# A streaming encoder step: expert rows are weighted out of PSUM and added onto the residual rows by indirect DMA

## What is computed

```
m = silu(c) @ w_ada + b                        # shift, scale, gate, for each request
h = LN0(x) * (1 + scale_m) + shift_m
x = LN_m(alpha * x + gate_m * mixer(h))        # "x1" below
h = LN0(x) * (1 + scale_f) + shift_f           # "h2" below
# each token: one of 4 groups, 2 of its 4 experts, weights w0 and w1
for e in range(16):
    a = silu(h @ w_gate[e]) * (h @ w_up[e])    # 1024 -> 512
    y = y + combine[:, e:e+1] * (a @ w_down[e])
x = LN_f(alpha * x + gate_f * y)               # gate_f: one row for prompt, one for sample
```

## Time and profile before

| | us |
|---|---|
| median of 3 runs | 1449.58 |
| the three runs | 1443.32, 1449.58, 1452.94 |
| the profiled execution, its own time | 1447.76 |
| its span | 1445.2 |

### The profile page before, as it was taken

The page is one execution under the profiler, slowest core; times in us unless marked ns, Lnnn a source line. Parts: engine busy times, 40 slices in busy tenths (PEclk is TensorE's granted clock), DMA queues, the critical chain, the costliest instruction groups (busy, mean ns, idle before and its releaser), DMA issues.

```text
span 1445.2 us, 19719 instructions
## 1 busy us (share of the span) xinstructions
PE 1286.7 (89%) x7193; PEld 994.2 (69%) x7194; DVE 799.4 (55%) x1042; ACT 589.2 (41%) x780; POOL 335.2 (23%) x449
## 2 busy tenths in 40 slices
PE   2897999999999989999999988999999999999900
PEld 0654678787787756656687876887777888887700
DVE  5624132323422065676689975556888251548678
ACT  0422012322212166676722132555777242447532
POOL 0122230001200065675535631000000000000073
PEclk8899999999999999999999998999999999999955
DMA  9755210102031171121323369666999261649773
GB/s 338 285 175 176 62 67 0 59 1 73 1 95 41 46 207 30 31 59 31 121 99 117 109 237 374 230 225 241 388 389 382 104 232 58 232 149 378 273 253 123
DMA packets 138775, 234.52 MB, mean 162 GB/s; under 512 B 57328, under 2 KB 58936, under 8 KB 138712
## 3 DMA queue, kind: packets, MB, share of 16 engines
q1 hardware_dynamic: 128440, 196.41, 38.6%
q0 software_dynamic: 6496, 23.60, 4.7%
q10 hardware_dynamic: 3776, 13.67, 2.3%
HBM read 197.96 MB, written 35.68 MB: 162 GB/s over the span
## 4 chain that ended last, share of the span: by engine, by line
PE 58%; issue 12%; DVE 8%; ACT 5%; POOL 5%; DMA 1%; ACTq 1%; POOLq 0%; DVEq 0%
PE psum L819 53%; POOL arena L2042 3%; PE psum L1025 2%; ACT high L1464 2%; PE psum L1214 1%; DVE arena L1981 1%; DVE arena L1980 1%; DVE arena L1973 1%; DVE arena L1971 1%; DVE arena L1972 1%; ACT a_high L1496 1%; PE psum L1220 1%; DMA arena<-h_rows,smalls 1%; DVE win_low L1676 0%; PE psum L1119 0%
## 5 line engine op out<-in xcount | busy, mean ns | idle before, releaser
L819 PE MATMUL psum<-win_high,x_high 128*128 128x512 f32 (+1 forms) x432 | 173.8, 402 | 3.5 <-DVE win_low L1676 3.5
L819 PE MATMUL psum<-win_high,x_low 128*128 128x512 f32 (+1 forms) x432 | 170.0, 394 | 0.0
L819 PE MATMUL psum<-win_low,x_high 128*128 128x512 f32 (+1 forms) x432 | 169.9, 393 | 0.0
L819 PE MATMUL psum<-arena 128*64 128x128 f32 (+9 forms) x1324 | 147.0, 379 | 24.6 <-DMA arena<-in_w_ada_mix 20.7
L819 PE MATMUL psum<-high,h_high 128*128 128x512 f32 x416 | 165.1, 397 | 2.5 <-DVE h_low L1927 2.5
L819 PE MATMUL psum<-high,h_low 128*128 128x512 f32 x416 | 163.2, 392 | 0.0
L819 PEld LDWEIGHTS psum<-arena 128*64 128x64 f32 (+6 forms) x1324 | 72.6, 143 | 75.1 <-issue 48.5
L1775 DVE TENSOR_TENSOR_SCAN arena<-arena,psum 128x512 f32<-128x512 f32 (+4 forms) x116 | 109.5, 978 | 19.6 <-ACT arena L1421 19.5
L1922 DVE TENSOR_TENSOR low_odd<-raw_odd,high 128x2048 fp32r<-128x2048 f32 x48 | 107.8, 2288 | 13.7 <-ACT high L1464 13.7
L1922 DVE TENSOR_TENSOR low_even<-raw_even,high 128x2048 fp32r<-128x2048 f32 x48 | 107.7, 2288 | 10.8 <-ACT high L1464 10.8
L2042 POOL TENSOR_TENSOR arena<-arena 128x512 f32<-128x512 f32 (+4 forms) x116 | 108.2, 932 | 9.3
(11 more groups left out here) (257 smaller groups left out, 2437.9 us busy)
## 6 DMA issues: line engine op xcount, KB each, us to landing
raw_even<-in_w_e_gate SPq DMA_DIRECT2D x8, 2048.0 KB, 11.0
raw_even<-in_w_e_up SPq DMA_DIRECT2D x8, 2048.0 KB, 16.5
raw_even<-in_w_e_down SPq DMA_DIRECT2D x8, 2048.0 KB, 14.7
raw_odd<-in_w_e_gate SPq DMA_DIRECT2D x8, 2048.0 KB, 10.5
raw_odd<-in_w_e_up SPq DMA_DIRECT2D x8, 2048.0 KB, 17.0
raw_odd<-in_w_e_down SPq DMA_DIRECT2D x8, 2048.0 KB, 15.1
win<-in_w_in SPq DMA_DIRECT2D x7, 2048.0 KB, 8.0
expert_rows<-arena ACTq DMA_DIRECT2D x26, 512.0 KB, 6.6
```

The source lines that it names most:

```text
L819: pe_last[0] = nc.tensor.matmul(*x, **y)
```

## The change

Parts of the diff, cut to its core. Expert loop, ACT, DVE and POOL:

```diff
@@ ACT, before the loop
+            act.wait_ge(s_ids, 2)
+            act.wait_ge(s_gi, 2)
+            A(slot_w.rearrange("p s b -> p (s b)"), bank(6)[:, 0:2 * MAX_BLOCKS], ACT.Copy).then_inc(s_gi, 1)
+            act.wait_ge(s_gi, 3)
             act.sem_inc(s_ye, 1)
-            act.sem_inc(s_ys, 16)
+            act.wait_ge(s_ys, 16)
+            act.wait_ge(s_router, 128)
@@ ACT, in each block, behind high_parts(nxt, (1, 2, 3))
+                        act.wait_ge(s_ye, b + 1)
+                        A(gate_rows, rows8[:, 1], ACT.Copy, scale=slot_w[:, 1, bass.ds(b, 1)]).then_inc(s_gsA, 1)
                         act.wait_ge(s_yp, b + 1)
-                        act.wait_ge(s_ys, 16 * b + 16)
-                        A(yb.rearrange("p (a c) -> p a c", a=2), psum[2][:], ACT.Copy).then_inc(s_ye, 1)
-                        act.wait_ge(s_ye, b + 2)
-                        act.dma_start(y_dram[bass.ds(b * P, P), :], yb).then_inc(s_ys, 16)
@@ DVE, in each block, behind low_parts(nxt, (1, 2, 3), before) and ahead of low_parts(nxt, (4, 5), before)
+                        dve.wait_ge(s_gsA, b + 1)
+                        STT(gate_rows, rows8[:, 0], slot_w[:, 0, bass.ds(b, 1)], gate_rows, ALU.mult, ALU.add).then_inc(s_gsD, 1)
+                        dve.wait_ge(s_gsD, b + 1)
+                        dve.wait_ge(s_yp, b + 1)
+                        dve.wait_ge(s_ys, 16 * b + 16)
+                        TT(yb, psum[2].rearrange("p a c -> p (a c)"), gate_rows, ALU.mult).then_inc(s_ye, 1)
@@ POOL
+            pool.indirect_dma_start(x1_dram, bass.IndirectOffsetOnAxis(ap=idc[:, 1:2], axis=0), gate_rows, None,
+                                    compute_op=ALU.add).then_inc(s_ys, 16)
             with pool.Fori(1, total + 1) as b:
                 pool.wait_ge(s_htr, b)
                 pool.wait_ge(s_hg, 16 * b)
-                pool.sem_inc(s_fill, 16)
-                G.tensor_copy(idc, gi[:, bass.ds(b, 1)]).then_inc(s_idx, 1)
-                pool.wait_ge(s_idx, b)
+                G.tensor_copy(idc[:, 0:1], gi[:, bass.ds(b, 1)]).then_inc(s_idx, 1)
+                pool.wait_ge(s_idx, 2 * b - 1)
                 pool.sem_inc(s_go, 1)
                 pool.indirect_dma_start(hg, None, h2_dram, bass.IndirectOffsetOnAxis(ap=idc[:, 0:1], axis=0)).then_inc(s_hg, 16)
+                pool.wait_ge(s_ys, 16 * b)
+                G.tensor_copy(idc[:, 1:2], si[:, bass.ds(b - 1, 1)]).then_inc(s_idx, 1)
+                pool.wait_ge(s_idx, 2 * b)
+                pool.wait_ge(s_ye, b + 1)
+                pool.sem_inc(s_go, 1)
+                pool.indirect_dma_start(x1_dram, bass.IndirectOffsetOnAxis(ap=idc[:, 1:2], axis=0), yb, None,
+                                        compute_op=ALU.add).then_inc(s_ys, 16)
```

```diff
@@ DVE, after w0 and w1, ahead of the ranks
+            step(TS(w18, w18, 1.0 / ALPHA, None, ALU.mult))
+            for part in range(3):
+                step(V.tensor_copy(w_part[part], w18 if part == 0 else w_rest))
+                if part < 2:
+                    step(TT(w_rest, w18 if part == 0 else w_rest, w_part[part], ALU.subtract))
@@ POOL, after the gather of block 0
+            for part in range(3):
+                w_of_token = w_part[part].unsqueeze(2).to_broadcast([P, 18, MAX_BLOCKS])
+                G.tensor_tensor(block_w[:, part], block_oh, w_of_token, ALU.mult).then_inc(s_bw, 1)
@@ SP
             sp.wait_ge(s_hg, 16)
+            sp.wait_ge(s_ids, 2)
...
-            with sp.Fori(total, MAX_BLOCKS) as b:
-                sp.dma_start(y_dram[bass.ds(b * P, P), :], zero_rows).then_inc(s_fill, 16)
```

Final stage: the 18 gathers, L1520, L1971, L1972, L1973 and the x1 loads go. SP loads the summed rows in four groups of tiles, (0), (1, 2), (3, 4, 5), (6, 7, 8), once the last add has landed:

```diff
+            sp.wait_ge(s_summed, 1)
+            for i, tiles in enumerate(SUM_GROUPS):
+                for t in tiles:
+                    sp.dma_start(ya[t][0:r], x1_dram[t * P:t * P + r, :]).then_inc(s_sum_in[i], 16)
@@ ACT
-                    A(ya[t][0:r], ya[t][0:r], ACT.Copy, scale=w0[0:r, t:t + 1]).then_inc(s_crs, 1)
+                    A(yc[t][0:r], ya[t][0:r], ACT.Copy, accum_out=fin_nm[0:r, t:t + 1]).then_inc(s_crs, 1)
```

```diff
+                    if j >= 2:
+                        keep_clock((8, 5)[j - 2], 4)
@@ PE, adasum
-                    if i >= 1:
-                        pe.wait_ge(s_rowo, i)
-                    mm(bank(6)[0:2, :], row_of_tile, ada_acc[:, i % 2], start=True, stop=True).then_inc(s_rsum, 1)
+                    if i >= 2:
+                        pe.wait_ge(s_rowo, i - 1)
+                    mm(bank(6 - 2 * (i % 2))[0:2, :], row_of_tile, ada_acc[:, i % 2], start=True, stop=True).then_inc(s_rsum, 1)
```

More of the change, by code:

```diff
@@ L550, in stream_step @@
         an = view(r_b + 17408, 2, 256)
-        zero_rows = view(r_m + EXPERT_W, D)
+        gate_rows = view(r_m + EXPERT_W, D)
+        block_w = view(r_b + 16384, 27 * MAX_BLOCKS).bitcast(BF16).rearrange("p (a n b) -> p a n b", a=3, n=18)
         ya = [view(r_b + D * t, D) for t in range(TILES)]
         yc = [view(r_a + D * t, D) for t in range(TILES)]
-        x1c = [view(r_m + D * t, D) for t in range(TILES)]
         rt = [r_tmp]
@@ L579, in stream_step @@
         dd = rtiny(9)
-        w0 = rtiny(9)
-        w1 = rtiny(9)
+        w01 = rtiny(2, 9)
+        w0, w1 = w01[:, 0], w01[:, 1]
+        w_rest = rtiny(18)
+        w_part = [rtiny(9).bitcast(BF16) for _ in range(3)]
+        slot_w = rtiny(2, MAX_BLOCKS)
         A0 = rtiny(9, 16)
@@ L824, in _, with keep_clock @@
             nc.tensor.transpose(bank(7)[:, 0:72], rows[0:72, :], ident[0:72, 0:72]).then_inc(s_rowT, 1)
+            def keep_clock(n, b=7):
+                for _ in range(n):
+                    mm(bank(b)[:, 0:256], ident, cst[:, 0:256], start=True, stop=True)
             pe.wait_ge(s_silu, 1)
@@ L1151, in _ @@
                     h2_turned(n - 2)
-            def keep_clock(n):
-                for _ in range(n):
-                    mm(bank(7)[:, 0:256], ident, cst[:, 0:256], start=True, stop=True)
             keep_clock(2)
@@ L1197, in _ @@
             pe.wait_ge(s_route, 1)
+            pe.wait_ge(s_gi, 2)
             block_turn(0)
+            for s in range(2):
+                tiles = [n for n in range(18) if (n % 9 == LAST) == bool(s)]
+                for part in range(3):
+                    pe.wait_ge(s_bw, part + 1)
+                    for n in tiles:
+                        r = rows_of(n % 9)
+                        last = mm(bank(6)[:, s * MAX_BLOCKS:(s + 1) * MAX_BLOCKS], place_oh[0:r, n, :], block_w[0:r, part, n, :],
+                                  start=(part == 0 and n == tiles[0]), stop=(part == 2 and n == tiles[-1]))
+            last.then_inc(s_ids, 1)
             with pe.Fori(0, EXPERTS // 2) as ee:
```

199 lines of the change are left out of this document (107 added, 92 removed).

## The result

The changed kernel takes 1554.11 us (median of 4 runs, 1551.86 to 1555.38) against 1447.74 for the kernel before beside it: ratio 1.0748, 95% interval 1.0713 to 1.0783. The forecast was 1487 and 1436 to 1535, so the direction was right and the size far too small. The profiled execution has a span of 1549.7, 104.5 more than before.

What follows compares the result with a forecast made beforehand. PE, busy 89% of the span, was taken to bound the kernel, except in first-projection waits and the 75.3 us after the expert loop. 1447.8 − 30 − 11 + 0 + 1 + 78 = 1485.8, about 1487 as median; range 1436 to 1535.

Steps and rivals of the forecast that it cites:

- the mechanism and its place: Expert loop: gather queued behind the add, which awaits s_ye; PE stalls 5.2 after each expert's last block, 15 times, +78.
- E: Rival in the expert loop: the accumulating DMA is slow, X near 13 everywhere, +166, total 1575; chance 7%.
- X: Expert loop: time from s_ye to the next gather's landing, 7.2 in quiet, taken as 9.7.
- I take 9.7, nearer to the quiet end, because a stall moves the weight loads away from the gather: Expert loop: the choice of X that gave a stall of 5.2, paid 15 times, +78.
- the upper end of 15: Expert loop: largest X, with slow issue twice (+2.9), loaded landing (+3.3) and 1.5 of the add ahead.
- rival D: Expert loop: PE's clock halves with the stalls, absorbed in runs of one-block experts, otherwise 30 more, 1517; chance 9%.
- DVE's longer chain: Expert loop: DVE's added operations cost 2.3 in each of ten one-block experts, 23 if nothing else were later.
- Final stage: −30 forecast: After the expert loop: 75.3 becomes about 45.5, DVE starting at 18.6, then 2.62 a tile; allowed −24 to −32.
- POOL (2.3) stays just under DVE: Final stage: POOL's scaling and power take 2.3 a tile, within DVE's 2.62, so DVE sets the pace.
- First projection: −11 forecast: Row sums: 13.9 of waits go, less a weight load 1.0 late 3 times; bounds −7 and −14.
- Start: 0: Start: reordered turns and projections give nothing; filler products return about 1.7 or cost about 1.6.
- Routing: +1: Routing: six more DVE operations of about 0.17 ahead of the first gather; range 0 to +3.

Runs made afterwards that it cites:

- experiment 1: Changed kernel with POOL's loop reordered, gathering the next block's rows before adding the finished block: 1427.46 us, ratio 0.9865 to the kernel before.
- experiment 8: Changed kernel with the next gather ahead of the add and the PSUM product ahead of the third low part: 1428.22 us, ratio 0.9878.
- experiment 9: Changed kernel with POOL's copy of the next gather's index made before the wait for s_ye, gather and add in their order: 1519.25 us, ratio 1.0518.
- experiment 2: Changed kernel with gate_rows and the PSUM product ahead of the next expert's third low part, in an expert's last block: 1494.5 us, ratio 1.0320.
- experiment 10: Changed kernel with ten filler products on PE before the wait at the turn, in each expert's first block: 1545.95 us, ratio 1.0690.
- experiment 4: Kernel before with only the change's start and first projection, including two banks and filler products: 1429.78 us, ratio 0.9876.
- experiment 11: Kernel before with only the two PSUM banks taking turns for the sums of rows: 1430.94 us, ratio 0.9897.
- experiment 12: Kernel before with the change's start and first projection but without the thirteen filler products: 1430.80 us, ratio 0.9903.
- experiment 6: Changed kernel with the next gather ahead of the add, and gate_rows finished on POOL instead of DVE: 1445.38 us, ratio 1.0003.

## Why the prediction was right and wrong

The error is 67 us: 1554 against 1487. Against the stages of the profile the forecast was −10 up to the loop (it was −13.1), +78 in the loop (+143.0), −30 in the final stage (−25.4), which makes 66.5 of it. Almost all is the loop.

**Right: the mechanism and its place.** The wait at the turn, 15 times, the gather right behind the add, s_ye 14 to 15 after the turn, the middle blocks unharmed. Experiments 1, 8 and 9 show it from three sides. (One rival was summed a little wrong: E's own terms make +168, not +166; nothing hangs on it.)

**Wrong: the size of X.** The step that failed is "I take 9.7, nearer to the quiet end, because a stall moves the weight loads away from the gather". For the seven stalls without a weight load it was good: X 10.3 and 11.1 where read, stalls of 5.05 on the mean against 5.2. For the eight with one X was 15.9 where read and 14.7 to 16.3 in all, around and over the upper end of 15 that I had worked out and weighed little. The stall doesn't move the loads away: they are issued once DVE and ACT have split the gates, ACT and DVE stand behind the same turn as everything else, and so loads and gather slide together; they were issued 0.12 us apart in the listing, and never more than 0.42. These eight hold 83.0 of the 118.3, where 8 × 5.2 = 41.6 were forecast; that is the whole of the 40 that the stalls hold too much. Each forecast row was there: the issue beside a big DVE operation (2.83), the index copy beside one (1.33 instead of 0.18, not in my sum), the landing among weight loads (10.6, where the earlier trace rows had 7.6 without the add on the same queue). Experiment 2 moved the gather 2.1 ahead of the loads and the landing fell to 6.7. That the loads have the larger part is read from this and from the last expert but one, which has none and 5.9. But in every gather that landed after 9.3 or more the issue was the long one and the load was issued before it was over (experiment 10: 1.0 behind its start, landed after 10.0). With an issue of 1.0 and the gate load 2.9 ahead of it, in the one-block experts of experiment 1, the gather landed after 7.0 to 8.7. So loads make up most of the way from 4.4 to 5.9 to there, and the last 1 to 3 come with the long issue among loads, which the forecast had as a longer issue and not as a later landing. How the two divide within one stall stays open: no run moved the loads alone or shortened the issue alone.

**Wrong: "in a run of one-block experts that is absorbed, since PE waits anyway".** The half clock was put down as a rival D with 9%; it is there behind all 15 stalls: the granted clock is 0.50 there, and full again 3 to 6 us after the turn began. These windows of 5 us show it around the turn of 1112.09 (granted clock third from the end):

```profile
1100.00:1105.00 5.00, 1.33 (x6) 0.76 (x5) 4.09 (x5) 0.00 (x0) 3.68 (x3) 1.00 0.93 168
1105.00:1110.00 5.00, 0.00 (x0) 0.00 (x0) 0.00 (x0) 0.00 (x0) 0.00 (x0) 0.53 1.02 362
1110.00:1115.00 5.00, 2.82 (x12) 2.42 (x12) 0.06 (x1) 0.43 (x2) 0.00 (x0) 0.50 1.01 368
1115.00:1120.00 5.00, 4.95 (x21) 4.14 (x22) 3.92 (x4) 5.00 (x5) 0.00 (x0) 0.95 0.40 150
```

PE fell from 2.4 to 1.2 GHz in its gap and came back about 3 us after it. It isn't absorbed, because the turn and the down products behind it are the head of the next chain: turn, splits, product, s_ye. The busy time between first product and last mark grew by 28.4 us, 1.9 a stall, and experiment 10 took 14.2 off the loop by keeping PE busy in the seven short gaps. The Trainium skill (TensorE: Matmul & The Clock Gate, "HAM oscillation — how this bites in real kernels") has it as the rule that a kernel with such a wait in every tile throttles in every tile, and this trace agrees. The loop's 143.0 is then 118.3 of stalls and 28.4 of half clock, less 3.7 of idle at other waits that the stalls covered.

**Right, DVE's longer chain.** It was put at 23 alone. Experiment 1, where the wait for the gather is gone, lost 17.7 in the loop, 17.1 of it in nine one-block steps.

**Final stage: −30 forecast, −25.4 measured**, in two terms. The timeline, counterpart of the earlier trace rows:

```profile
1500.10 1.23 DVE L2023 TENSOR_TENSOR arena<-psum,arena 128x1024 f32<-128x1024 f32 x1 [2.44 <-PE psum L831]
1502.14 1.60 POOL L2172 DMA_INDIRECT x_rows<-arena,smalls  x1 [12.91 <-DVE arena L2023]
1508.31 4.41 SPq L812 DMA_DIRECT2D arena<-x_rows  x9
1518.96 1.28 DVE L2036 SCALAR_TENSOR_TENSOR arena<-arena,smalls 128x1024 f32<-128x1024 f32 x1 [17.64 <-POOL smalls L2188]
1522.31 1.29 DVE L2036 SCALAR_TENSOR_TENSOR arena<-arena,smalls 128x1024 f32<-128x1024 f32 x1 [0.74 <-POOL smalls L2188]
1522.56 1.09 POOL L2187 TENSOR_SCALAR smalls<-smalls 128x1 f32<-128x1 f32 x1
1523.64 1.28 DVE L2037 SCALAR_TENSOR_TENSOR arena<-arena,smalls 128x1024 f32<-128x1024 f32 x1
1523.73 1.61 POOL L2188 TENSOR_TENSOR smalls<-smalls 128x1 f32<-128x1 f32 x1
1525.38 1.28 DVE L2036 SCALAR_TENSOR_TENSOR arena<-arena,smalls 128x1024 f32<-128x1024 f32 x1 [0.46 <-POOL smalls L2188]
```

DVE begins at 19.1 against the forecast 18.6, and that this is near is luck. The forecast's own terms, 9.6 + 4 × 1.34 + 2.3, make 17.3 and not 18.6. The add needs 6.2 from issue to SP's load and not 4.3, so ACT's first copy starts at 11.9 and not 9.6, and ACT stands another 1.5 before the second; against that, scaling and power for tile 0 took 0.19 and 0.57, with DVE still at rest, and not 2.3. Then a tile takes 3.07 instead of 2.62, because "POOL (2.3) stays just under DVE" was wrong: its scaling, 0.19 with DVE at rest, takes 1.09 beside L2036, which the 2.3 did not have, and its power 1.61 instead of 0.57 beside L2037, which it had. The scaling ends when DVE's operation ends and the power 0.4 after the next one; POOL is held up beside DVE and then DVE waits for POOL. Nine tiles by 0.45 are 4.0, and 0.5 was late before them.

**First projection: −11 forecast, about −14.** The weight load that was to be late 3 times for 1.0 shows 0.2 in all, the last line (up to 2.2 in three waits in experiment 2, with the same start); the other is the wait that was 3.5:

```profile
PE psum L831 <- DVE win_low L1731: 3.9, 1, 3.9
PE psum L831 <- DMA arena<-in_w_ada_ffn: 0.2, 1, 0.2
```

**Start: 0**, and no difference is seen: experiments 4, 11 and 12 lie within 1.2 us. **Routing: +1** is not tested: the first marks of the change and of experiment 4 are 1.7 apart, less than the scatter. Around ACT's new wait for the rows8 loads PE shows a single wait of 0.2, for DVE at the turn L1258 of the first block.

## What to carry to other kernels

Where one in-order queue carries both a result going out and data coming in, issue the incoming one first: the same operations in the other order are worth 127 us here. When a stall is priced, ask what else hangs on the stalled event: what does moves with it, and meets the late transfer again in every round; and price the half clock behind each gap. Read what is left of a change when its accident is removed: with the order mended, expert rows added by DMA gain 25 us at the end, lose 18 in the loop, and leave 1427.5 against 1429.8 for the start's part alone, which is not a difference; and of the start's part, two PSUM banks taking turns are all that a run could show.

## What the runs showed of the hardware

- Tiny GpSimd operations stretch beside VectorE's large ones, to where those end or a little past it: 0.19 to 1.09 and 0.57 to 1.61 for 128x1 operands, an index copy 0.18 to 1.33, an indirect DMA's issue 1.00 to 2.83. It works the other way too: three low parts, 6.70 alone, took 8.92 beside POOL's own 1024-column operations (experiment 6). The Trainium skill (SBUF — State Buffer, "SBUF: two separate sides") gives the lock between the two engines' ports; these rows agree.
- An accumulating indirect DMA of 512 KB lands in 7.4 us, the same rows written in 4.6; its issue takes 2.32 against 1.72 on the mean (2.85 and 2.25 beside DVE's low parts, 1.60 and 1.00 away from them).
- The same gather lands 4.4 to 5.9 us after the start of its issue in the seven stalls with no weight load close behind it. With a 2 MB load issued 2.1 behind it landed in 6.7 (issue 2.23, experiment 2), at 1.4 behind in 7.6 (issue 1.28, experiment 9), at 0.12 behind in 10.6 (issue 2.83), and at 1.0 behind in 10.0 (issue 2.83, experiment 10). With the load 2.9 ahead and an issue of 1.0 it landed in 7.0 to 8.7 (experiment 1, one-block experts).
- The granted clock over the first 100 us was 0.95 in the changed kernel's profile and 0.91 in those of experiments 2 and 10, with the same code there; the first expert product came 6 us later in the two.
